# Keeping the partition sums of a conditioning matrix-vector product and finishing them in two batches

## What is computed

```
c_act = silu(c)                                   # [1, 2048]
for l in range(2):
    mod = c_act @ w_mod[l] + b_mod[l]             # [1, 6144]
    shift, scale, gate = split(mod, 3)
    h = x * (1 + scale) + shift
    y = attention_l(h)                            # for l = 1 with shared keys and values
    x = layer_norm(ALPHA * x + gate * y)
kv_mod = c_act @ kv_w_mod + kv_b_mod              # [1, 4096], shift and scale of the shared keys and values
```

## Time and profile before

| | |
|---|---|
| median of 3 runs | 2598.83 us (2597.77 to 2602.55) |
| span of the profiled execution | 2599.7 us; no other time of it is given |
| TensorE busy | 2554.0 us, 98% |
| VectorE busy | 1803.6 us, 69% |
| ScalarE busy | 1154.6 us, 44% |
| DMA | 605.74 MB, 233 GB/s in the mean |
| small products (L696) | 7.4 us busy in 64 halves |

### The profile page before, as it was taken

One profiled execution on the slowest core, in us unless ns is written; L12 is line 12 of the kernel. 1 busy time (PEld: TensorE's weight loads), 2 busy tenths in 40 slices (PEclk: granted clock), 3 DMA queues, 4 the chain that ended last, 5 costly groups with the idle time before them and its releaser, 6 DMA issues.

```text
span 2599.7 us, 38429 instructions
## 1 busy us (share of the span) xinstructions
PE 2554.0 (98%) x14550; PEld 2156.5 (83%) x14550; DVE 1803.6 (69%) x2342; ACT 1154.6 (44%) x1475; POOL 0.2 (0%) x4
## 2 busy tenths in 40 slices
PE   8999999999999999999999999999999999999998
PEld 8977878778888888888888888899987778999886
DVE  6897676776667777777776666776786665545756
ACT  5454333445544544444443334333486344334642
POOL 0000000000000000000000000000000000000000
PEclk9999999999999999999999999999999999999999
DMA  6777676776768888888887777888845546675464
GB/s 212 247 236 247 210 249 216 255 255 211 251 227 271 270 276 276 270 272 278 277 276 250 251 253 258 280 275 275 257 138 189 186 159 181 185 230 178 137 215 143
DMA packets 317949, 605.74 MB, mean 233 GB/s; under 512 B 27742, under 2 KB 31844, under 8 KB 316140
## 3 DMA queue, kind: packets, MB, share of 16 engines
q1 hardware_dynamic: 301628, 571.59, 68.3%
q10 hardware_dynamic: 16176, 32.15, 3.6%
HBM read 593.03 MB, written 10.62 MB: 232 GB/s over the span
## 4 chain that ended last, share of the span: by engine, by line
PE 90%; DVE 4%; DMA 2%; ACT 2%; issue 2%; SPq 0%; ACTq 0%; DVEq 0%
PE bank L661 22%; PE bank L663 22%; PE bank L662 22%; PE bank L688 5%; PE bank L686 5%; PE bank L687 5%; DMA gemv_w<-in_w_mod 2%; PE bank L604 2%; PE bank L787 1%; DVE gemv_acc L1927 1%; DVE w_lo L1908 1%; DVE conv_out L2056 1%; ACT w_hi L1281 1%; PE bank L1120 1%; PE bank L813 0%
## 5 line engine op out<-in xcount | busy, mean ns | idle before, releaser
L1908 DVE TENSOR_TENSOR w_lo<-raw,w_hi 128x1024 fp32r<-128x1024 f32 x820 | 1001.7, 1223 | 725.9 <-ACT w_hi L1281 723.9
L1281 ACT CAST w_hi<-raw 128x1024 fp32r<-128x1024 f32 x820 | 859.3, 1049 | 1347.1 <-PE bank L663 1001.7
L661 PE MATMUL bank<-w_hi,u_hi 128*128 128x512 f32 x1216 | 491.9, 404 | 6.3 <-issue 3.8
L663 PE MATMUL bank<-w_hi,u_lo 128*128 128x512 f32 x1216 | 481.2, 396 | 0.0
L662 PE MATMUL bank<-w_lo,u_hi 128*128 128x512 f32 x1216 | 480.9, 395 | 0.0
L1927 DVE SCALAR_TENSOR_TENSOR gemv_acc<-gemv_w,small,gemv_acc 128x512 f32<-128x512 f32 x480 | 357.9, 746 | 23.2 <-DMA gemv_w<-in_w_mod 21.9
L661 PE MATMUL bank<-w_hi,s_hi 128*128 128x512 f32 x744 | 300.9, 404 | 1.3 <-DVE w_lo L1908 1.2
L663 PE MATMUL bank<-w_hi,s_lo 128*128 128x512 f32 x744 | 294.2, 395 | 0.0
L662 PE MATMUL bank<-w_lo,s_hi 128*128 128x512 f32 x744 | 294.2, 395 | 0.0
L688 PE MATMUL bank<-s_hi,w_lo 128*128 128x256 f32 x1024 | 290.1, 283 | 0.0
L687 PE MATMUL bank<-s_lo,w_hi 128*128 128x256 f32 x1024 | 289.5, 283 | 0.0
(11 more groups left out here) (362 smaller groups left out, 2882.6 us busy)
## 6 DMA issues: line engine op xcount, KB each, us to landing
gemv_w<-in_w_mod SPq DMA_DIRECT2D x384, 256.0 KB, 3.2
raw<-in_w_in SPq DMA_DIRECT2D x176, 512.0 KB, 4.5
raw<-in_a_w_in SPq DMA_DIRECT2D x128, 512.0 KB, 4.5
raw<-in_w_ffn_gate SPq DMA_DIRECT2D x88, 512.0 KB, 4.6
raw<-in_w_ffn_up SPq DMA_DIRECT2D x88, 512.0 KB, 4.4
raw<-in_w_ffn_down SPq DMA_DIRECT2D x88, 512.0 KB, 4.3
gemv_w<-in_kv_w_mod SPq DMA_DIRECT2D x128, 256.0 KB, 3.5
raw<-in_kv_w SPq DMA_DIRECT2D x64, 512.0 KB, 3.7
```

Source lines behind the costliest of these rows:

```text
L661: pe.matmul(o, xh, w_hi[:, s, t], start=(k == 0), stop=False)
L663: ins = pe.matmul(o, xl, w_hi[:, s, t], start=False, stop=(k == 2 * units - 1))
L1281: act.copy(w_hi[:, s], raw[:, s]).then_inc(hi_done, 1)
L1908: dve.tensor_tensor(w_lo[:, s], raw[:, s], w_hi[:, s].bitcast(F32), ALU.subtract).then_inc(lo_done, 1)
```

## The change

The reduced sums of chunks 0 to 21 are kept side by side in a larger `gemv_sums`; nothing is done on TensorE and ScalarE in the bodies. At unit 3 of down (TensorE, behind the transposes that stand there already) three products take 8, 8 and 6 chunks, that is 128, 128 and 96 weight columns; at unit 5 ScalarE copies twice and stores three times. The load of rows 0 to 47 moves from unit 0 to unit 9 of ScalarE's stream. Chunks 22 to 31 go into the same tile from its start; VectorE waits for the first batch once, before the reduce of chunk 22. They are finished by two products of 5 chunks (80 columns) at slot 1 of g2, one copy and two stores at slot 3.

```diff
+MOD_FIRST, MOD_REST = 22, 10
...
-        gemv_sums = place("gemv_sums", [P, COLS // SQ], F32)
-        gemv_row = place("gemv_row", [P, SQ], F32)
+        gemv_sums = place("gemv_sums", [P, MOD_FIRST, COLS // SQ], F32)
+        gemv_row = place("gemv_row", [P, 2, SQ], F32)
+        gemv_last = place("gemv_last", [P, SQ], F32)
...
+            pr.mod_kept = MOD_FIRST if mod0 >= MOD_FIRST else 0
...
+        BATCH = P * SQ // COLS
+        REST = MOD_REST // 2
...
-            def mod_reduce(n, b=MODB):
-                pe.wait_ge(gemv_cut, n * 2 + 2)
-                pe.matmul(bank[b][0:COLS // SQ, 0:SQ], gemv_sums[:], quads[:], start=True, stop=True).then_inc(mod_sum, 1)
-            def mod_due(pr, i, j):
-                m = mod_part(pr, i, j, 5)
-                if m is not None and not (isinstance(i, int) and i * pr.mods + mod_base(pr, i) + m == 0):
-                    mod_reduce(i * pr.mods + (mod_base(pr, i) + m - 1))
+            def mod_sums(b, n0, chunks, col):
+                lhs = gemv_sums[:, n0:n0 + chunks].rearrange("p n s -> p (n s)")
+                return pe.matmul(bank[b][0:chunks * COLS // SQ, col:col + SQ], lhs, quads[:], start=True, stop=True)
+            def first_mods():
+                pe.wait_ge(gemv_cut, 2 * MOD_FIRST)
+                mod_sums(MODB, 0, BATCH, 0)
+                mod_sums(MODB, BATCH, BATCH, SQ)
+                mod_sums(MODB, 2 * BATCH, MOD_FIRST - 2 * BATCH, 2 * SQ).then_inc(mod_sum, 1)
+            def rest_of_mods():
+                pe.wait_ge(gemv_cut, 2 * MOD_CHUNKS)
+                mod_sums(PROBS_T, 0, REST, 0)
+                mod_sums(PROBS_T, REST, REST, SQ).then_inc(mod_sum, 1)
...
                 if j == 3:
                     turn_stage(pr, pr.bodies - 1, 1)
+                    first_mods()
...
-            def mod_copy(n, b=MODB):
-                act.wait_ge(mod_sum, n + 1)
-                act.copy(gemv_row[0:COLS // SQ], bank[b][0:COLS // SQ, 0:SQ]).then_inc(mod_copied, 1)
-                act.wait_ge(mod_copied, n + 1)
-                dst = mods[ds(n * 4, 4), :].rearrange("r (q c) -> (r q) c", c=SQ)
-                act.dma_start(dst, gemv_row[0:COLS // SQ]).then_inc(mod_stored, 16)
+            def first_mods():
+                act.wait_ge(mod_sum, 1)
+                act.copy(gemv_row[:].rearrange("p b c -> p (b c)"), bank[MODB][:, 0:2 * SQ]).then_inc(mod_copied, 1)
+                last = (MOD_FIRST - 2 * BATCH) * COLS // SQ
+                act.copy(gemv_last[0:last], bank[MODB][0:last, 2 * SQ:3 * SQ]).then_inc(mod_copied, 1)
+                act.wait_ge(mod_copied, 2)
+                for b in range(2):
+                    act.dma_start(mod_rows_of(b * BATCH, BATCH), gemv_row[:, b]).then_inc(mod_stored, 16)
+                act.dma_start(mod_rows_of(2 * BATCH, MOD_FIRST - 2 * BATCH), gemv_last[0:last]).then_inc(mod_stored, 16)
...
-                act.wait_ge(mod_stored, 16 * ((r1 * P) // COLS))
+                act.wait_ge(mod_stored, (48, 80)[n])
...
-                    if i == 0 and j == 0:
+                    if i == 0 and j == 5:
+                        first_mods()
+                    if i == 0 and j == 9:
                         mod_rows_in(0)
...
-                    if not (isinstance(i, int) and i * pr.mods + n == 0):
-                        dve.wait_ge(mod_stored, i * (pr.mods * 16) + 16 * n)
-                    dve.tensor_reduce(gemv_sums[:], gemv_t[:].rearrange("p (b c) -> p b c", c=SQ), AX.X, ALU.add).then_inc(
-                        gemv_cut, 1)
+                    if isinstance(i, int) and i * pr.mods + n == MOD_FIRST:
+                        dve.wait_ge(mod_sum, 1)
+                    dve.tensor_reduce(gemv_sums[:, ds(i * pr.mods + (n - pr.mod_kept), 1)].rearrange("p n s -> p (n s)"),
+                                      gemv_t[:].rearrange("p (b c) -> p b c", c=SQ), AX.X, ALU.add).then_inc(gemv_cut, 1)
```

More of the change, by code:

```diff
@@ L394, in block_kernel @@
         MOD_CHUNKS = MOD_COLS // COLS
-        assert mod0 == MOD_CHUNKS
+        assert mod0 == MOD_CHUNKS and MOD_FIRST + MOD_REST == MOD_CHUNKS
+        BATCH = P * SQ // COLS
+        REST = MOD_REST // 2
         def without_mod(pr, i):
@@ L708, in due @@
                 def due(j):
-                    mod_due(pr, i, j)
                     if between:
@@ L1161, in due @@
                             pe.wait_ge(turn_free, pr.ahead0)
-                            mod_reduce(MOD_CHUNKS - 1, PROBS_T)
+                            rest_of_mods()
                         for h in heads_at(p, slot, 0):
@@ L1169, in due @@
                                 pe.wait_ge(turn_free, pr.ahead0)
-                                pe.wait_ge(mod_copied, MOD_CHUNKS)
+                                pe.wait_ge(mod_copied, 3)
                             turn_probs(p, h, work[:, parts * h % 4])
@@ L1200, in _ @@
             pe.wait_ge(signal("lam_exp"), 1)
-            pe.wait_ge(mod_copied, MOD_CHUNKS - 1)
+            pe.wait_ge(mod_copied, 2)
             def wide_heads(o, f, th):
@@ L1301, in nothing, with mod_rows_of, rest_of_mods @@
                 pass
-            def mod_copy(n, b=MODB):
-                act.wait_ge(mod_sum, n + 1)
-                act.copy(gemv_row[0:COLS // SQ], bank[b][0:COLS // SQ, 0:SQ]).then_inc(mod_copied, 1)
-                act.wait_ge(mod_copied, n + 1)
-                dst = mods[ds(n * 4, 4), :].rearrange("r (q c) -> (r q) c", c=SQ)
-                act.dma_start(dst, gemv_row[0:COLS // SQ]).then_inc(mod_stored, 16)
[L1311 to L1314, removed]
+            def mod_rows_of(n0, chunks):
+                return mods[n0 * 4:(n0 + chunks) * 4, :].rearrange("r (q c) -> (r q) c", c=SQ)
+            def first_mods():
[7 more added lines that the diff above has]
+                act.dma_start(mod_rows_of(2 * BATCH, MOD_FIRST - 2 * BATCH), gemv_last[0:last]).then_inc(mod_stored, 16)
+            def rest_of_mods():
+                rows_used = REST * COLS // SQ
+                act.wait_ge(mod_sum, 2)
+                act.copy(gemv_row[0:rows_used].rearrange("p b c -> p (b c)"), bank[PROBS_T][0:rows_used, 0:2 * SQ]).then_inc(
+                    mod_copied, 1)
+                act.wait_ge(mod_copied, 3)
+                for b in range(2):
+                    act.dma_start(mod_rows_of(MOD_FIRST + b * REST, REST), gemv_row[0:rows_used, b]).then_inc(mod_stored, 16)
             def hi_of_turn(n, parity, dst, scale_col=None, banks=(TURN, TURN + 1)):
@@ L1813, in between @@
                         if p == "d" and slot == 3:
-                            mod_copy(MOD_CHUNKS - 1, PROBS_T)
+                            rest_of_mods()
                         for c in range(parts):
```

## The result

| | before | changed |
|---|---|---|
| median of five runs each, us | 2598.83 (2597.77 to 2602.55) | 2554.89 (2551.59 to 2558.18) |
| ratio to before | | 0.983 (0.9819 to 0.984) |
| profiled span, us | 2599.7 | 2556.4 |

(Executions last about 1.8 us longer than their spans: 2558.18 for the one with 2556.4. The page of the kernel before doesn't show this.)

The account below looks back on a forecast made before the run. TensorE was taken to bound the kernel outside the first 172 us. From the median 2598.83 us, 9.8 removed and 0.7 added gave 2589.7 us, with a range of 2585.5 to 2596 to hold 8 in 10.

Parts of the forecast that it names:

- TensorE as the bound: Whole kernel: TensorE busy 2554.0 of 2599.7 us, others paced by it; its savings outside the first stretch shorten the end.
- Price of a small product: L696 products between wide or across matmuls: each adds 0.36 us, half the product, the rest paid on entering and leaving.
- Removed 9.8, added 0.7, sum 9.1 us: TensorE's stream: small products removed save 9.8 us, the two batches add 0.7, so 9.1 us come off the median.
- the entry of 0.1: In both batches: 0.1 us added for entering the 96-column product, and 0.1 for the 80-column ones.
- Waits, ScalarE, the moved load of mod_rows: TensorE's waits before the batches, ScalarE's copies and issues, and the load moved to unit 9: all priced at 0.
- The 0.36 hidden in qkv: One small product at 132.9 us, where the chain holds no TensorE work: its 0.36 us was taken out as hidden.
- The address shift: Everything placed above the larger tiles moves by 1600 bytes, to 64 past a multiple of 256: priced at 0.
- Rival B: Shifted region read more slowly in k2, q2, k3, q3: 3.1 us per ns of matmul, 2608.1 at 6 ns; chance 0.07.
- A: Gain absorbed as TensorE waits for casts or weights: 2591.6 us if partly, 2598.8 to 2599.5 if wholly; chance 0.12.
- C: Another penalty appears where narrow products stood, such as the unit's semaphore wait; only 4.3 us gained, 2594.5; chance 0.05.
- D: Batches dearer, through a TensorE stall or ScalarE delaying a cast: 3 us, 2592.7; chance counted within the forecast's 0.76.
- The extra transaction: DMA gates<-spill into the moved region: a 2 KB row off 256 bytes takes a ninth transaction, an estimated 0.8 us.

Follow-up runs that it names:

- work_again: The changed kernel with its larger tiles at the end of the partition, so region is back at its old address: 2588.75 us, ratio to before 0.9964.
- shift64: The kernel before with region moved by 64 bytes and nothing else changed: 2563.84 us, ratio to before 0.9862.
- shift_again: The kernel before with 1600 unused bytes ahead of region and nothing else changed, measured a second time: 2564.57 us, ratio to before 0.9866.
- after_back64: The changed kernel with gemv_last put at the end, so region lies 64 bytes lower at 105728, a multiple of 256: 2587.81 us, ratio to before 0.9948.
- steps_alone: A separate kernel repeating the wide and across matmul units on constant data at eight operand distances, other engines idle or loaded: 686.79 us.

## Why the prediction was wrong, point by point

- **TensorE as the bound**: right. A saving in its stream came off the end.
- **Price of a small product, 0.36 us, on entry and exit**: right, 45.86 - 45.50 = 0.36 in a body.
- **Removed 9.8, added 0.7, sum 9.1 us**: right as the price of the change's work. `work_again` measured 9.4 (two earlier runs 13 to 14, with wide intervals), and the traces 8.0 where the same prices give 7.7. The batches cost 0.62 and about 0 us; the entry of 0.1 that the sum gave to the halves with 96 and 80 columns isn't paid.
- **Waits, ScalarE, the moved load of mod_rows**: priced at 0; TensorE waits before neither batch, and the sum holds. None was tested by itself.
- **The 0.36 hidden in qkv**: its stretch is unchanged, but 0.4 us is below what the runs can tell.
- **"The address shift ... I price it at 0"**: this step failed, and it is the whole miss, 35 us. The reason given was that a wide and an across matmul stream 512 columns in the same 0.24 us though their moving operands lie at different places within 256 bytes. That compares the wrong thing. What counts is the distance between the two operands of one matmul, and both rows are from one kernel, in which it is 128 for both; the stationary operand, which is what the shift moves under the wide matmuls, was not considered. A trace with one distance can't show what another would do, and rows to 10 ns can't show 3 ns: at distance 128 the two rates aren't even equal, 232.4 ns and 2 x 118.7 = 237.4. So the cost had to be bounded from both sides, and only a loss was.
- **Rival B** came nearest: it had the time of a step depend on where region lies. But it had the wrong sign, spoke of the place of the moving operand by itself and not of its distance to the other one, and left out the wide matmuls, which bring more than half. It was no forecast of a gain.
- **Rivals A, C and D** did not occur. TensorE's waits for w_lo are 5.4 us before, 7.0 in the changed kernel and 4.7 in `work_again`, not several us more (A); the ffn body falls by the whole 0.36, so no seam is left (C); the batches cost less than 0.7 (D).
- The extra transaction that the prediction took from the Trainium skill ("DMA: Bandwidth & Descriptors", section "How a descriptor splits into AXI transactions"), an estimated 0.8 us, did not show: ScalarE's wait for gates<-spill is 6.6 us before, and 6.7, 6.9 and 7.0 in the changed kernel, `shift64` and `shift_again`, where region is off a multiple of 256, but 8.1 and 8.5 in `work_again` and `after_back64`, where it is on one.

## What to carry to other kernels

When an edit changes the size of a tile, look at what moves behind it: here 64 unused bytes were worth almost four times the edit itself. Where TensorE is the bound, test a few relative places of stationary and moving operand (here 0 and 192 of 256 bytes were good; 0 is the best for wide matmuls and among the worst for across ones), and compare an edit with the old addresses kept, or its price is mixed with theirs. Read a change of steps from landmarks hundreds of matmuls apart.

## What the runs showed of the hardware that was not expected

The time from one float32 matmul to the next depends on the places of stationary and moving operand relative to each other within 256 bytes: 227.2 to 234.2 ns for 512 columns and 113.4 to 119.9 ns for 256, at a granted clock of 0.998 (2.4 GHz) and with all other engines idle. It isn't symmetric: 192 is good and 64 is not. Why is open, and that two reads get in each other's way is an inference; only steps of 32 bytes, one weight width and this alternation of three operands were tried. The Trainium skill ("TensorE: Matmul & The Clock Gate", section "Part 2: What happens when you issue a matmul") says that the engine has two independent read ports and that loading the next weights takes no read bandwidth from the running matmul. If the two reads were independent in every respect, the steps of `steps_alone` would be equal; they differ by up to 6%, so for these matmuls the measurement decides.

Whether a small product pays the entry of 0.09 us goes with its weight columns. Behind a wide matmul (L663) in the kernel before, a product with 16 weight columns (L696, 27 times) and one with 64 (L787, 19 times) start after 0.32 to 0.33 us; transposes with 128 columns after 0.23 in the median. In the changed kernel the product with 80 columns starts after 0.23. The border lies between 64 and 80 columns here; the products with 64 columns also had only 64 rows, so the two aren't separated.
